# Two-layer hybrid backbone on one core: half of the streamed modulation chunks summed on VectorE, and the router product turned round

## The reference

```
cond_lat = silu(c);  cond_ctx = silu(c_ctx)
m  = cond_lat @ w_ada[layer] + b_ada[layer]     # w_ada[layer]: 1024 x 6144
mc = cond_ctx @ w_ada[layer] + b_ada[layer]
sh1, sc1, g1, sh2, sc2, g2 = split(m, 6)
y = parallel_mixers(layer_norm(x) * (1 + sc1) + sh1, ...)   # input projection, Fourier, attention, pooling, gating, output projection
x = layer_norm(alpha * x + g1 * y)
h2 = layer_norm(x) * (1 + sc2) + sh2
logits = h2 @ [w_router_group | w_router_expert]            # 1024 x (4 + 32)
x = layer_norm(alpha * x + g2 * experts(h2, logits))        # top-1 group, top-2 experts in it
```

## Time and profile before

| | us |
|---|---|
| median of three executions | 2670.03 (2668.91 to 2671.3) |
| profiled execution: its own time | 2669.63 |
| profiled execution: span | 2667.7 |
| PE busy | 2358.7 (88% of the span) |
| DVE busy | 838.9 (31%) |
| ACT busy | 435.9 (16%) |
| POOL busy | 481.8 (18%) |

### The profile page before, as it was taken

One profiled execution on the slowest core, in us unless ns is written; L12 is line 12 of the kernel. 1 busy time (PEld: TensorE's weight loads), 2 busy tenths in 40 slices (PEclk: granted clock), 3 DMA queues, 4 the chain that ended last, 5 costly groups with the idle time before them and its releaser, 6 DMA issues. The chain is left out here.

```text
span 2667.7 us, 39347 instructions
## 1 busy us (share of the span) xinstructions
PE 2358.7 (88%) x15384; PEld 1651.4 (62%) x15384; DVE 838.9 (31%) x2103; ACT 435.9 (16%) x1079; POOL 481.8 (18%) x608
## 2 busy tenths in 40 slices
PE   4999879999299999999959997999489999999975
PEld 3999745565166666666638984555266666666642
DVE  1323345655601111011115665465611111011107
ACT  0010132321011111111101112222001111111111
POOL 0000003444111111111111111344111111111114
PEclk8999989999599999999979998899689999999997
DMA  9454420001397999999932103100189999999945
GB/s 357 148 177 145 181 94 26 24 17 48 131 369 296 391 399 392 389 391 395 369 114 100 48 33 117 59 17 24 57 356 384 384 381 393 386 389 381 372 191 202
DMA packets 130511, 608.74 MB, mean 228 GB/s; under 512 B 20608, under 2 KB 23680, under 8 KB 111984
## 3 DMA queue, kind: packets, MB, share of 16 engines
q1 hardware_dynamic: 112400, 569.61, 54.8%
q0 software_dynamic: 16864, 37.78, 3.8%
q10 hardware_dynamic: 1152, 0.03, 0.0%
HBM read 599.41 MB, written 42.04 MB: 240 GB/s over the span
## 5 line engine op out<-in xcount | busy, mean ns | idle before, releaser
L1888 PEld LDWEIGHTS gate_up<-room,w_gate_up 128*128 128x128 f32 x4608 | 522.6, 194 | 31.5 <-issue 31.5
L1888 PE MATMUL gate_up<-room,w_gate_up 128*128 128x128 f32 x4608 | 529.4, 277 | 3.1 <-DVE room L1795 3.1
L1897 PE MATMUL down<-w_down,room 128*128 128x512 f32 x576 | 256.8, 599 | 0.0
L1905 PE MATMUL gate_up_short<-w_gate_up,room 128*64 128x512 f32 x1152 | 255.1, 595 | 0.0
L1804 DVE TENSOR_TENSOR room<-room,gate_up 128x128 f32<-128x128 f32 x144 | 41.4, 287 | 599.3 <-ACT room L1823 599.3
L1905 PEld LDWEIGHTS gate_up_short<-w_gate_up,room 128*64 128x64 f32 x1152 | 79.5, 137 | 171.2 <-issue 171.2
L1897 PEld LDWEIGHTS down<-w_down,room 128*128 128x128 f32 x576 | 106.5, 190 | 123.0 <-issue 120.5
L1807 DVE TENSOR_TENSOR room<-room,gate_up_short 128x256 f32<-128x256 f32 x36 | 15.2, 421 | 495.1 <-ACT room L1829 495.1
L1515 POOL COPY rows_idx<-slot_token 128x1 int32 (+1 forms) x78 | 14.3, 183 | 792.6 <-PE rows_turned L1875 712.0
L1918 PE MATMUL down<-w_down,room 128*64 128x512 f32 x576 | 131.5, 598 | 11.9 <-ACT room L1831 11.9
L1337 PE MATMUL proj<-w_out,mixT 128*128 128x512 f32 x288 | 129.5, 592 | 0.0
(11 more groups left out here) (354 smaller groups left out, 3213.3 us busy)
## 6 DMA issues: line engine op xcount, KB each, us to landing
w_gate_up<-in_w_exp_gate SPq DMA_DIRECT2D x72, 2048.0 KB, 8.6
w_gate_up<-in_w_exp_up SPq DMA_DIRECT2D x72, 2048.0 KB, 13.3
w_down<-in_w_exp_down SPq DMA_DIRECT2D x72, 2048.0 KB
ada_w<-in_w_ada SPq DMA_DIRECT2D x48, 1024.0 KB, 7.1
h_rows<-h SPq DMA_DIRECT2D x18, 512.0 KB, 2.6
w_out<-in_w_out SPq DMA_DIRECT2D x2, 4096.0 KB, 14.1
w_in<-in_w_in SPq DMA_DIRECT2D x2, 3072.0 KB, 17.5
xn<-expert_rows SPq DMA_DIRECT2D x10, 512.0 KB, 4.0
```

The costliest lines, as they stand in the source:

```text
L1888: mm = nc.tensor.matmul(H[j % 2][:, o, :], wgu[0][:, o, k, j * P:(j + 1) * P], xT[0][:, k, :], start=k == 0, stop=k == KT - 1)
L1897: mm = nc.tensor.matmul(Y[:, h, :], hid[:, j, :], wd[0][:, j, h * 512:(h + 1) * 512], start=j == 0, stop=j == JT - 1)
L1905: mm = nc.tensor.matmul(Hs[c * HP:(c + 1) * HP, :, :], xT[1][:, k, :], wgu[1][:, :, k, c * 2 * P:(c + 1) * 2 * P], start=k == 0, stop=k == ...
```

## The change

Part one is in `project_first`. Of the 20 chunks behind the lead, every second one (`by_dve`) is no longer multiplied on PE. `sum_chunk` on DVE multiplies each row block by the condition value of its partition and adds up, 16 operations of 128x512 for both streams, into `acc` (128 x 2 x 512). `add_rows` on PE then sums over the 128 partitions with a constant 128x2 matrix as weights: 2 streams x 4 column tiles, 8 matmuls. Chunks now come in PC = 4 parts of 512 KB, into NW = 5 buffers, each with a semaphore of its own for "used".

Part two is in `attend`. The router weights become the weights of the matmul (128x36), and `hT` moves (128 columns). Even row blocks go to the column tile at partition 0, odd ones to that at partition 64, so that two half sums lie turned in `turn`. ACT copies both to `lt`, and one matmul with `lt` as weights and `fold` (two identities on top of each other) moving adds the halves and turns them back; the copy to `logits` moves behind it, into the next step.

```
-    NC, HK, NW, LEAD = 6 * D // 512, KT // 2, 3, 4
+    NC, PC, NW, LEAD = 6 * D // 512, 4, 5, 4
+    HK = KT // PC
+    by_dve = lambda c: c >= LEAD and (c - LEAD) % 2 == 1
+        acc, pick = sb("ada_sum", [P, 2, 512]), sb("stream_of", [P, 2, 2])
@@ sync @@
-                chunks(LEAD, CHUNKS)
+                for t in range(NT):
+                    for c in (LEAD + 2 * t, LEAD + 2 * t + 1):
+                        for h in range(PC):
+                            chunk_part(PC * c + h)
+                    for c in (LEAD + 2 * t, LEAD + 2 * t + 1):
+                        chunk_bias(c)
+                    if t:
+                        chunk_store(LEAD + 2 * t - 2)
+                        chunk_store(LEAD + 2 * t - 1)
+                chunk_store(CHUNKS - 2)
                 chunk_store(CHUNKS - 1)
@@ vector @@
+                def sum_chunk(c):
+                    if c > LEAD + 1:
+                        v.wait_ge(added, (c - LEAD) // 2)
+                    for h in range(PC):
+                        n = PC * c + h
+                        v.wait_ge(wa_in[n % NW], n // NW * 16 + 16)
+                        for k in range(HK):
+                            for i in range(2):
+                                w_k, by = wa[n % NW][:, k, :], act_c[:, h * HK + k, i:i + 1]
+                                if h == 0 and k == 0:
+                                    op = nc.vector.tensor_scalar(acc[:, i, :], w_k, by, None, ALU.mult)
+                                else:
+                                    v.wait_ge(s.sem, s.at() - 1)
+                                    op = nc.vector.scalar_tensor_tensor(acc[:, i, :], w_k, by, acc[:, i, :], ALU.mult, ALU.add)
+                                op.then_inc(s.sem, s.up())
+                        v.wait_ge(s.sem, s.at())
+                        nc.vector.engine_nop().then_inc(wa_used[n % NW], 1)
+                    nc.vector.engine_nop().then_inc(acc_done, 1)
...
                     if t + 2 < NT:
                         normalise(t + 2)
+                    if t:
+                        add_bias(LEAD + 2 * t - 1)
+                    sum_chunk(LEAD + 2 * t + 1)
                     v.wait_ge(c_done, t + 1)
...
-                    for c in range(PER):
-                        add_bias(LEAD + t * PER + c)
+                    add_bias(LEAD + 2 * t)
+                add_bias(CHUNKS - 1)
@@ tensor @@
+                def add_rows(c):
+                    pe.wait_ge(acc_done, (c - LEAD) // 2 + 1)
+                    pe.wait_ge(m_read, c - 1)
+                    for i in range(2):
+                        for j in range(4):
+                            mm = nc.tensor.matmul(M[c % 2][32 * j:32 * j + 2, 0:P], pick[:, i, :], acc[:, i, j * P:(j + 1) * P], start=i == 0, stop=i == 1)
+                    mm.then_inc(added, 1)
...
                     if t + 1 < NT:
                         turn(t + 1)
-                    for c in range(PER - 1):
-                        chunk(LEAD + t * PER + c)
+                    if t:
+                        add_rows(LEAD + 2 * t - 1)
+                    chunk(LEAD + 2 * t)
...
-                    chunk(LEAD + t * PER + PER - 1)
+                add_rows(CHUNKS - 1)
@@ attend, scalar @@
+                def logits(u):
+                    b, n = turn_of["router", u, 0, 0]
+                    act.wait_ge(T_full[b], n + 1)
+                    nc.scalar.activation(g.logits[:, u, :], T[b][:, 1, 0:NR], ACT.Copy).then_inc(T_read[b], 1)
                 for t in range(N + 2):
+                    if t >= 3:
+                        logits(t - 3)
...
                     if rtr(t):
-                        act.wait_ge(T_full[b], n + 1)
-                        nc.scalar.activation(g.logits[:, t - 2, :], T[b][:, 0, 0:NR], ACT.Copy).then_inc(T_read[b], 1)
+                        act.wait_ge(r_full, t - 1)
+                        for o in (0, HD):
+                            nc.scalar.activation(lt[o:o + NR, :], T[b][o:o + NR, 0, :], ACT.Copy).then_inc(lt_ready, 1)
+                logits(N - 1)
@@ attend, tensor @@
                     for k in range(KT):
-                        mm = nc.tensor.matmul(T[b][:, 0, 0:NR], hT[:, k, :], wr[:, k, :], start=k == 0, stop=k == KT - 1)
-                    mm.then_inc(T_full[b], 1)
+                        o = k % 2 * HD
+                        mm = nc.tensor.matmul(T[b][o:o + NR, 0, :], wr[:, k, :], hT[:, k, :], start=k < 2, stop=k >= KT - 2)
+                    mm.then_inc(r_full, 1)
+                def router_rows(u):
+                    b, n = turn_of["router", u, 0, 0]
+                    pe.wait_ge(lt_ready, 2 * u + 2)
+                    nc.tensor.matmul(T[b][:, 1, 0:NR], lt[:, :], fold[:, :], start=True, stop=True).then_inc(T_full[b], 1)
                 for t in range(N + 2):
                     if att(t):
                         scores(t, 0)
+                    if t >= 3 and t != N:
+                        router_rows(t - 3)
...
                     if t == N:
                         router(N - 3)
+                        router_rows(N - 3)
...
+                router_rows(N - 1)
```

More of the change, by code:

```diff
@@ L269, in project_first @@
         c_in, k_in, x0_in, silu_done = sem("c_in"), sem("consts_in"), sem("x_first_in"), sem("silu_done")
-        wa_in, wa_used, bias_in = [sem(f"ada_w_in{i}") for i in range(NW)], sem("ada_w_used"), [sem(f"ada_bias_in{i}") for i in range(2)]
+        wa_in, wa_used, bias_in = [sem(f"ada_w_in{i}") for i in range(NW)], [sem(f"ada_w_used{i}") for i in range(NW)], [sem(f"ada_bias_in{i}") for i in range(2)]
+        added, acc_done, picks = sem("ada_added"), sem("ada_summed"), sem("picks_set")
         m_read, stored, cols_in, scaled = sem("ada_read"), [sem(f"mods_stored{i}") for i in range(2)], sem("cols_in"), sem("cols_scaled")
@@ L304, in chunks @@
                     for c in range(lo, hi):
-                        chunk_half(2 * c)
+                        chunk_part(PC * c)
                         chunk_bias(c)
-                        chunk_half(2 * c + 1)
+                        for h in range(1, PC):
+                            chunk_part(PC * c + h)
                         if c > lo:
@@ L329, in _ @@
             def _(pool):
+                nc.gpsimd.memset(pick[:, :, :], 0.0).then_inc(picks, 1)
+                pool.wait_ge(picks, 1)
+                for i in range(2):
+                    nc.gpsimd.memset(pick[:, i, i:i + 1], 1.0).then_inc(picks, 1)
                 for lo, hi in ((0, PAD), (PAD + SEQ, PL + PAD), (PW - PAD, PW)):
@@ L358, in modulate @@
                     i.then_inc(mod_v, 1)
+                def sum_chunk(c):
[16 more added lines that the diff above has]
+                    nc.vector.engine_nop().then_inc(acc_done, 1)
                 def add_bias(c):
-                    v.wait_ge(wa_used, 2 * c + 2)
+                    if by_dve(c):
+                        v.wait_ge(added, (c - LEAD) // 2 + 1)
+                    else:
+                        v.wait_ge(wa_used[(PC * c + PC - 1) % NW], (PC * c + PC - 1) // NW + 1)
                     v.wait_ge(bias_in[c % 2], c // 2 * 16 + 16)
@@ L439, in _, with chunk_part @@
             def _(pe):
-                def chunk_half(n):
-                    c, h = n // 2, n % 2
+                def chunk_part(n):
+                    c, h = n // PC, n % PC
                     pe.wait_ge(wa_in[n % NW], n // NW * 16 + 16)
@@ L447, in chunk_half @@
                             mm = nc.tensor.matmul(M[c % 2][32 * j:32 * j + 2, 0:P], act_c[:, h * HK + k, :], wa[n % NW][:, k, j * P:(j + 1) * P],
-                                                  start=h == 0 and k == 0, stop=h == 1 and k == HK - 1)
-                    mm.then_inc(wa_used, 1)
+                                                  start=h == 0 and k == 0, stop=h == PC - 1 and k == HK - 1)
+                    mm.then_inc(wa_used[n % NW], 1)
                 def chunk(c):
-                    chunk_half(2 * c)
-                    chunk_half(2 * c + 1)
+                    for h in range(PC):
+                        chunk_part(PC * c + h)
+                def add_rows(c):
+                    pe.wait_ge(acc_done, (c - LEAD) // 2 + 1)
+                    pe.wait_ge(m_read, c - 1)
+                    if c == LEAD + 1:
+                        pe.wait_ge(picks, 3)
+                    for i in range(2):
+                        for j in range(4):
+                            mm = nc.tensor.matmul(M[c % 2][32 * j:32 * j + 2, 0:P], pick[:, i, :], acc[:, i, j * P:(j + 1) * P], start=i == 0, stop=i == 1)
+                    mm.then_inc(added, 1)
                 def turn(t):
```

16 lines of the change are left out of this document (11 added, 5 removed).

## The result

| | before | after |
|---|---|---|
| median of the runs of the first comparison | 2669.47 (2667.54 to 2671.3, 4 runs) | 2639.14 (2638.64 to 2641.03, 4 runs) |
| median over all later runs too | 2667.1 (2660.9 to 2672.3, 69 runs) | 2639.8 (2636.0 to 2643.2, 14 runs) |
| profiled execution, span | 2669.63, 2667.7 | 2639.44, 2637.6 |
| PE, DVE busy | 2358.7, 838.9 | 2328.2, 942.3 |

The ratio is 0.9892 (0.9877 to 0.9908): 30.3 us less in the first comparison, 27.3 by the medians over all runs.

What follows compares the result with a forecast made beforehand. PE was taken to bound projection and attend. Gains of 11.5 (projection) and 9.7 us (attend), 21.2 together, off 2669.63 gave 2648.4, plus 0.4 for the median 2648.8, called 2649; own range 2644 to 2654, 8-in-10 range 2643 to 2658.

Steps and rivals of the forecast that it cites:

- the price of the context router: Layer 0 attend's first context step: at 1.2 GHz router 1.8 plus `router_rows` 0.3 us against 3.3, gain 1.1 us.
- the tail's 0.4: End of attend, last router and what follows it at the lower clock: gain 0.4 us in each layer, 0.8 in all.
- The steady routers: Attend's steady loop: router 0.95 plus `router_rows` 0.24 us against 1.90, gain 0.71 each, 7.8 us for eleven.
- The projection: First projection stage: end at 305.4 us for 316.86, gain 11.5 us, bounds 9 and 13.
- the 288.0 of the working: Last projection tile: time in us at which PE would reach its `add_rows`, from 301.27 less nine chunks plus eight `add_rows`.
- The last sum: End of the projection: DVE's uncovered sum of 16 operations, claimed to take 10.2 us and end at 300.0.
- the two of 0.60 us: DVE in the projection: two 128x512 operations starting 0.60 us apart, taken as the sum's spacing, 9.6 us for 16.
- the pair that was set aside as dependent (0.74): DVE: two dependent operations starting 0.74 us apart, used only for the sum's upper bound, 11.8 us, and the pipe drains.
- The rule quoted beside it: DVE's sum: next operation starts only once the pipe is empty, so spacing at least 0.69 us, sum about 11.5.
- 1: Projection: DVE becomes the bound, 1.30 us an operation, 30.7 us a tile; about 2714 us; 4 in 100.
- 2: Attend: column tiles don't run side by side, or waits eat the gain; 0 to -2 for 9.7; 2659 us; 10 in 100.
- 3: Projection: quarters starve the lead or the tiles, 1 us per lead chunk, some 0.5 per tile; 2658 us; 10 in 100.

Runs made afterwards that it cites:

- filled_wait: The kernel before, with two matmuls of unused result in PE's 1.87 us wait of the context step; 2664.08 us (0.9991).
- one_column_tile: The changed kernel, with all eight router products on column tile 0 and one identity turning the one copy; 2651.73 us (0.994).
- last_chunk_on_tensor: The changed kernel, with the projection's very last chunk back on PE; 2636.04 us (0.9875).
- filled_tail: The kernel of `last_chunk_on_tensor`, with nine idle matmuls in the 4.44 us wait ahead of each attend's last turn; 2642.08 us (0.9904).
- last_chunk_again: The kernel of `last_chunk_on_tensor` run and profiled a second time, no further edit; 2636.28 us (0.9888).
- longer_sum: The changed kernel, with 24 operations for 16 in each DVE sum; 2729 us, with tokens sent to other experts and 4864 expert matmuls for 4608.
- quarters_alone: The kernel before, with chunks in four quarters and five buffers for two halves and three, all chunks on PE; 2666.07 us (0.999).

## Why the prediction was too high

- **The step that failed** is the price of the context router, "so 1.8 + 0.3 against 3.3: 1.1 us" (by these terms it is 1.2). It let the lower clock stand as a given of that place. The wait did stay at 1.87 us, but behind it the clock stayed at 1.00 in all four profiles of the changed kernel. The step and the stretch behind it gave 3.8 us where 1.5 had been forecast, the tail's 0.4 among them: `filled_wait` shows that 3.1 of them are the clock, 0.6 are the shorter router, and 0.1 is the tail. Why the clock stays up is open. It isn't the router's length (`one_column_tile`) or the wait, which is equal, and the form of the router alone isn't it either: the kernel of `last_chunk_on_tensor` has the new form, and its clock fell in one profile and stayed up in the other. `filled_tail`, which fell, and `last_chunk_again`, which didn't, have the same instructions up to there and the same chip; what is seen to differ is when they come to this place. So some of the 3.1 us may be luck; how often the changed kernel has the lower clock there, in its unprofiled runs too, is not shown.
- **The steady routers** gave 0.81 us each, not 0.71. The router itself was right (0.98 us for 0.95, `router_rows` 0.24). The value product ahead of it takes 1.09 us from start to start and not 1.19: before, a product with 128x128 weights followed the one with 64 columns, and now weights of 36 columns follow (1.10 in `one_column_tile` too). Over eleven that is 1.0 us.
- **The projection** was forecast at 11.5 and gave 11.0, out of errors that cancel. PE came to the last tile's `add_rows` at 285.33, 2.7 us ahead of the 288.0 of the working. Of these, 1.8 are a period of 24.57 for 24.8: a chunk that goes takes 0.1 us with it from bank D ahead of it (1.78 us for 1.88 to the next start) and 0.1 from bank A behind it (3.58 for 3.67), beside its own 1.86; `add_rows` took 0.43 for 0.47. The rest is the lead and the first tile. The last sum took 10.7 us for 10.2 and waited 2.1 for a late quarter, which was not forecast, and so ended at 299.98, where the working had 300.0. That these met is luck. The operations of the sum stood 0.69 to 0.71 us apart. Their nearest row was taken to be the two of 0.60 us, which are statistics that read one operand; the pair that was set aside as dependent (0.74) was the right kin. The rule quoted beside it (the Trainium skill, "VectorE: DVE Perf Modes", section "The DRAIN you can't avoid") had the spacing of these 14 right, and its sum of 11.5 only missed that the first two operations, with one tensor operand, take 0.40 each. The spacing cost 0.5 us at the end of the stage.
- **The rivals.** 1: DVE keeps 4.1 us of slack in a tile; 8 more operations made it the bound (`longer_sum`). 2: refuted by 61 ns. 3: refuted by `quarters_alone`.
- **What no step could have held.** 4.6 us come from stretches that the change doesn't touch, above all 4.2 us before layer 1's `transform`, shown but not explained. And 2.4 us come from a kernel before whose first four runs lay high. The two overlap, since its profiled executions lay high as well. The stages that are touched hold 2.8 of the 9.9 us between forecast and time: 2.3 are the clock and the tail of layer 0, 1.0 the steady routers and the tail of layer 1, and the projection takes 0.5 back. The range was too narrow for it: it knew only bounds from the parts of the change, and nothing of how far a stage moves that is not changed.

## What to carry to other kernels

Where a stretch runs at the lower clock behind a wait of PE, don't take the clock as given: price the stretch at both levels, and look at more than one profile, since one kernel showed both here. A few idle matmuls in the wait, no more than it holds, gave 1.97 us at each of two places. Where weights of at most 64 columns change with every product, alternate two column tiles: it took the router from 1.84 to 0.98 us. And give a change of 1% a range that holds the drift of the stages it leaves alone, here some 4 us.

## What the hardware showed that was not expected

- Behind one wait of PE of 1.87 us the granted clock fell to 0.50 in one profile of a kernel and stayed at 1.00 in another profile of the same kernel; the lower clock cost 3.3 us there.
- Instructions of two column tiles started 6 to 7 ns apart, each tile's own 109 ns apart, with all 128 rows in both.
- Two operations of 128x512 with one tensor operand took 0.79 us together, 14 with two operands 0.71 each.
- One and the same descriptor issue on SP took 0.42 or about 2.1 us, depending on the kernel around it, and the loads behind it came 2.9 us later.
